# GLU products of a conformer and gMLP mixer in split float32r parts, their low parts made by VectorE between the taps of a depthwise convolution

## The reference

```python
z = h @ w_in + b_in
a = z[..., :2 * D_CONV]
uv = z[..., 2 * D_CONV:2 * D_CONV + 2 * D_GMLP]
gates = jax.nn.sigmoid(z[..., 2 * D_CONV + 2 * D_GMLP:])
a = jax.nn.glu(a, axis=-1)
a_full = jnp.concatenate([conv_hist.astype(a.dtype), a], axis=1)
...
a = jax.nn.silu(layer_norm(depthwise_causal_conv(a_full, conv_w, conv_b), ln_g, ln_b))
y_a = a @ w_a
uv = jax.nn.gelu(uv)
u, v = uv[..., :D_GMLP], uv[..., D_GMLP:]
v = layer_norm(v, v_ln_g, v_ln_b)
y_b = spatial_gate(u, v, w_s, b_s) @ w_b
merged = gates[..., :D_MODEL] * y_a + gates[..., D_MODEL:] * y_b
```

## Time and profile before

| | before |
|---|---|
| median of 3 runs | 967.47 us (964.45 to 967.98) |
| the profiled execution: span from first to last instruction | 963.2 us |
| mean granted TensorE clock, share of full speed | 0.940 |
| TensorE busy (matmuls) | 845.6 us, 88% of the span |
| VectorE busy | 509.0 us, 53% |
| ScalarE busy | 190.9 us, 20% |
| GpSimd busy | 168.8 us, 18% |
| 240 taps of the convolution (line 1280) | 175.1 us of VectorE |
| 512 plain GLU products (line 552) | 119.1 us of TensorE |

### The profile page before, as it was taken

The page is one execution under the profiler, slowest core; times in us unless marked ns, Lnnn a source line. Parts: engine busy times, 40 slices in busy tenths (PEclk is TensorE's granted clock), DMA queues, the critical chain, the costliest instruction groups (busy, mean ns, idle before and its releaser), DMA issues. The chain is left out here.

```text
span 963.2 us, 12133 instructions
## 1 busy us (share of the span) xinstructions
PE 845.6 (88%) x4994; PEld 618.5 (64%) x4994; DVE 509.0 (53%) x753; ACT 190.9 (20%) x284; POOL 168.8 (18%) x156
## 2 busy tenths in 40 slices
PE   2899999999998879979999999917999987979776
PEld 1688886347997879978878644605666655545432
DVE  1328999999999443351365543481333331222236
ACT  3211211111233121741120011201111110101003
POOL 1000000000045454143223000001122221121110
PEclk9899999999998889989999999856999998989899
DMA  9923225011332131365999593242999999999936
GB/s 323 315 64 88 65 67 174 1 44 44 89 88 57 48 88 45 88 219 175 316 314 322 186 381 149 97 193 83 411 404 416 415 418 394 368 406 394 373 110 248
DMA packets 112600, 204.16 MB, mean 212 GB/s; under 512 B 9484, under 2 KB 68212, under 8 KB 104350
## 3 DMA queue, kind: packets, MB, share of 16 engines
q1 hardware_dynamic: 94192, 159.36, 46.5%
q10 hardware_dynamic: 12830, 34.93, 9.6%
q0 software_dynamic: 5520, 9.06, 2.5%
HBM read 199.49 MB, written 14.84 MB: 223 GB/s over the span
## 5 line engine op out<-in xcount | busy, mean ns | idle before, releaser
L858 PE MATMUL PS<-arena 128*64 128x256 f32 (+1 forms) x1056 | 148.7, 411 | 30.2 <-issue 25.7
L1280 DVE SCALAR_TENSOR_TENSOR arena<-arena,VT 128x574 f32<-128x574 f32 x240 | 175.1, 811 | 0.0
L858 PEld LDWEIGHTS PS<-arena 128*64 128x64 f32 (+1 forms) x1056 | 108.8, 156 | 65.4 <-issue 36.9
L1695 POOL TENSOR_TENSOR wL<-arena,wH 128x1024 fp32r<-128x1024 f32 x32 | 83.2, 2621 | 360.8 <-ACT wH L998 360.8
L552 PE MATMUL PS<-arena 128*128 128x272 f32 x512 | 119.1, 396 | 1.6 <-DVE arena L1242 1.6
L552 PEld LDWEIGHTS PS<-arena 128*128 128x128 f32 x512 | 98.3, 192 | 22.1 <-issue 1.6
L619 PE MATMUL PS<-gH,wH 128*128 128x272 f32 x384 | 83.0, 299 | 9.1 <-POOL wL L1695 5.5
L1591 DVE TENSOR_TENSOR arena<-PS,arena 128x256 f32<-128x256 f32 x19 | 8.1, 424 | 140.1 <-ACT arena L1114 140.1
L619 PE MATMUL PS<-gL,wH 128*128 128x272 f32 x384 | 81.9, 296 | 0.0
L619 PE MATMUL PS<-gH,wL 128*128 128x272 f32 x384 | 81.7, 294 | 0.0
L878 PE MATMUL PS<-arena 128*64 128x512 f32 (+1 forms) x264 | 69.1, 597 | 1.4 <-DVE arena L1595 1.4
(11 more groups left out here) (282 smaller groups left out, 996.9 us busy)
## 6 DMA issues: line engine op xcount, KB each, us to landing
arena<-w_gate SPq DMA_DIRECT2D x32, 1024.0 KB, 7.3
arena<-w_up SPq DMA_DIRECT2D x32, 1024.0 KB, 15.4
arena<-w_down ACTq DMA_DIRECT2D x28, 1024.0 KB, 13.9
arena<-w_in SPq DMA_DIRECT2D x40, 512.0 KB, 5.2
arena<-w_ada SPq DMA_DIRECT2D x8, 2048.0 KB, 14.4
vecs<-w_ada SPq DMA_DIRECT2D x4, 2048.0 KB, 9.3
arena<-x_prompt SPq DMA_DIRECT2D x8, 512.0 KB, 8.0
arena<-w_in SPq DMA_DIRECT2D x4, 1024.0 KB, 6.3
```

The costliest lines, as they stand in the source:

```text
L858: last = pe.matmul(PS[h * rows:(h + 1) * rows, 2, n * DE:(n + 1) * DE], hG[:, b, k * SLOTS + h * rows:k * SLOTS + (h + 1) * rows], buf[r / ...
L1280: dve.scalar_tensor_tensor(out=total, in0=src, scalar=tap, in1=total, op0=ALU.mult, op1=ALU.add).then_inc(conv_step, 1)
L1695: pool.tensor_tensor(wL2[q % 2][:, m], WP[q % 2][:, m], wH2[q % 2][:, m], ALU.subtract).then_inc(gw_split, 1)
```

## The change

The GLU units become split products like the u units. ScalarE makes their weight high parts (high_of with the new semaphore a_high) and VectorE their low parts (low_a, a_split). VectorE now scales all eight tiles of hT, and the input's high parts (ScalarE) and low parts (VectorE) are made at the start, tile by tile; TensorE's unit 0 follows them step by step. The low parts of units 3 to 7 stand at fixed taps of the convolution's first pair (A_AT), those of the u units at fixed taps of pairs 4 and 6 (U_AT). The scratch row of the bias split moves to another buffer.

```diff
             for n in range(KT):
                 b = n % 2
-                full(pe, U_A + n)
                 pe.wait_ge(act_drained, Q_A + n - 1)
-                for m in range(2):
-                    last = product(4 * b + 2 * m, WP[b][:, m], hT, first=(n == 0))
+                if n == 0:
+                    for m in range(2):
+                        pe.wait_ge(a_split, m + 1)
+                    for k in range(KT):
+                        pe.wait_ge(g_high, k + 1)
+                        for w, part in ((wH2, gH), (wL2, gH), (wH2, gL)):
+                            if part is gL:
+                                pe.wait_ge(g_split, k + 1)
+                            for m in range(2):
+                                for h in range(2):
+                                    last = pe.matmul(PS[:, 2 * m + h, 0:H], w[0][:, m, k, :], part[:, k, h * H:(h + 1) * H],
...
+                else:
+                    for m in range(2):
+                        pe.wait_ge(a_split, 2 * n + m + 1)
+                        last = product_split(4 * b + 2 * m, wH2[b][:, m], wL2[b][:, m], gH, gL)
                 last.then_inc(w_used, 1)
...
-            act.wait_ge(s1_ready, 1)
-            for j in range(1, KT, 2):
...
+            def high_of(n, signal):
+                full(act, n)
+                for m in range(2):
+                    act.activation(wH2[n % 2][:, m], WP[n % 2][:, m], ACT.Copy).then_inc(signal, 1)
+
+            high_of(U_A, a_high)
+            for j in range(KT):
+                act.wait_ge(h_scaled, 2 * j + 2)
+                act.activation(gH[:, j, :], hT[:, j, :], ACT.Copy).then_inc(g_high, 1)
...
+            high_of(U_A + 1, a_high)
             act.wait_ge(start_dr, 3)
             act.wait_ge(aF_written, 4)
             for n in range(KT):
...
-                if n == 2:
-                    act.wait_ge(h_even, KT)
-                    act.wait_ge(h_odd, KT)
-                    act.wait_ge(bias_split, 3)
-                if n in (2, 3, 4, 5):
-                    for j in (2 * n - 4, 2 * n - 3):
-                        act.activation(gH[:, j, :], hT[:, j, :], ACT.Copy).then_inc(g_high, 1)
...
+                if n < KT - 2:
+                    high_of(U_A + n + 2, a_high)
...
+            def low_h(j):
+                dve.wait_ge(g_high, j + 1)
+                dve.tensor_tensor(gL[:, j, :], hT[:, j, :], gH[:, j, :], ALU.subtract).then_inc(g_split, 1)
+
+            def low_a(n):
+                for m in range(2):
+                    dve.wait_ge(a_high, 2 * n + m + 1)
+                    dve.tensor_tensor(wL2[n % 2][:, m], WP[n % 2][:, m], wH2[n % 2][:, m], ALU.subtract).then_inc(a_split, 1)
+
+            scale_h(0)
+            low_a(0)
+            scale_h(1)
+            for j in range(KT):
+                if j + 2 < KT:
+                    scale_h(j + 2)
+                low_h(j)
+            low_a(1)
...
+            low_a(2)
+            A_AT = {5: 3, 12: 4, 18: 5, 25: 6, 30: 7}
+            U_AT = {(4, 14): 0, (4, 24): 1, (6, 4): 3}
             for i in range(0, KT, 2):
+                if i == 6:
+                    low_u(2)
...
-                    if i == 6 and k in (9, 17, 25):
-                        low_u((k - 1) // 8)
-                if i == 2:
-                    dve.wait_ge(g_high, KT)
-                    for j in range(KT):
-                        dve.tensor_tensor(gL[:, j, :], hT[:, j, :], gH[:, j, :], ALU.subtract).then_inc(g_split, 1)
-                if i == 4:
-                    low_u(0)
+                    if i == 0 and k in A_AT:
+                        low_a(A_AT[k])
+                    if (i, k) in U_AT:
+                        low_u(U_AT[i, k])
```

More of the change, by code:

```diff
@@ L190, in build @@
         mg, sqj = tmp2[:, 0, 0:D], tmp2[:, 1, 0:D]
+        piece = mg[0:1, :]
         histR = tmp2[:, 1, 0:D]
@@ L545, in _ @@
         def _(pe):
-            def product(bank, tile_w, act, first=False):
-                for k in range(KT):
-                    if first:
-                        pe.wait_ge(h_odd if k % 2 else h_even, 2 * (k // 2 + 1))
-                    for h in range(2):
-                        last = pe.matmul(PS[:, bank + h, 0:H], tile_w[:, k, :], act[:, k, h * H:(h + 1) * H],
-                                         start=(k == 0), stop=(k == KT - 1))
-                return last
             pe.wait_ge(consts, NCONST)
@@ L625, in _ @@
                 b = n % 2
-                full(pe, U_A + n)
                 pe.wait_ge(act_drained, Q_A + n - 1)
-                for m in range(2):
-                    last = product(4 * b + 2 * m, WP[b][:, m], hT, first=(n == 0))
+                if n == 0:
[9 more added lines that the diff above has]
+                                    last = pe.matmul(PS[:, 2 * m + h, 0:H], w[0][:, m, k, :], part[:, k, h * H:(h + 1) * H],
+                                                     start=(k == 0 and w is wH2 and part is gH), stop=(k == KT - 1 and part is gL))
+                else:
+                    for m in range(2):
+                        pe.wait_ge(a_split, 2 * n + m + 1)
+                        last = product_split(4 * b + 2 * m, wH2[b][:, m], wL2[b][:, m], gH, gL)
                 last.then_inc(w_used, 1)
@@ L1239, in _, with scale_h @@
             dve.wait_ge(xt_copied, TT)
-            for j in range(0, KT, 2):
+            def scale_h(j):
                 for s, (c0, c1) in enumerate(((0, NPROMPT), (NPROMPT, T))):
                     dve.tensor_scalar(hT[:, j, c0:c1], hT[:, j, c0:c1], S1[:, s, j:j + 1],
-                                      VT[:, COL_MOD + 2 * j + s:COL_MOD + 2 * j + s + 1], ALU.mult, ALU.add).then_inc(h_even, 1)
+                                      VT[:, COL_MOD + 2 * j + s:COL_MOD + 2 * j + s + 1], ALU.mult, ALU.add).then_inc(h_scaled, 1)
+            def low_h(j):
[13 more added lines that the diff above has]
+            low_a(1)
             dve.wait_ge(bc_in, 64)
             then(dve.memset(b3, 0.0))
-            rest, piece = bvb[0:1, :], mod1[0:1, 0:D]
+            rest = bvb[0:1, :]
             for r in range(3):
```

24 lines of the change are left out of this document (9 added, 15 removed).

## The result

Four runs of the changed kernel gave a median of 988.15 us (985.83 to 989.42), four of the kernel before 967.73 us (964.45 to 969.45). The ratio is 1.0213, with a 95% interval of 1.0189 to 1.0236. The prediction was 986.8 us (975 to 992), slower.

A forecast was written before the change was run, and what follows sets the result against it. VectorE's gapless stream was taken to bound the kernel from 75 to 317 us. Terms 4.6 + 11.35 - 5.17 + 4.3 + 4.2 gave +19.3 us, span 982.5, plus 4.3 to the median: 986.8 us, range 975 to 992.

The forecast's parts named there:

- TensorE's gain: GLU units on TensorE: each falls from 14.9 to 12.1 us, 22 us over eight units, which TensorE then waits away.
- Rival (c): Whole kernel: not slower, TensorE sets the end and its lead comes through, 957.6 us; chance 0.05.
- The start: Up to the first GLU products: unit 1 comes late, so the convolution begins at 79.7 instead of 75.06, +4.6 us.
- The step that I weighed most: ScalarE's queue at the start: eight DMA issues, 8.9 us, delay unit 1's high part; TensorE idles 4.3 us.
- rival (b): Start: ScalarE's DMA issues hold nothing up, convolution begins 6 to 7 us earlier, about 980 us; chance alone 0.10.
- The five pieces: First pair of VectorE's convolution: low weights of units 3 to 7 between the taps, 2.27 us each, +11.35 us.
- The inputs' low parts: Between the second and third pair of the convolution: they leave VectorE's stretch there, -5.17 us.
- The waits: VectorE at u units 1 to 3: waits for ScalarE's high parts, 2.2, 0.6 and 1.5 us, together +4.3 us.
- GpSimd beside the additions: After the taps: four held GpSimd products meet VectorE's additions, 13.84 us instead of 9.65, +4.2 us.
- Rival (a): Convolution: GpSimd's products are done beneath the taps at no cost to VectorE, 978.5 us; chance 0.17.
- What TensorE gains before 290 us, it waits away: TensorE up to the mixes: it runs ahead of VectorE, so its gains there end in waits; no size of its own.
- the distance of 4.3 us between span and median: Whole kernel: the median 967.47 lies 4.3 us above the profiled span 963.2; kept, it turns 982.5 into 986.8.

The follow-up runs named there:

- E10: Changed kernel with GLU units 3 to 7 as plain products again, without the five low-weight pieces, u places at later taps; 969.54 us, ratio to before 1.0035.
- E1: Changed kernel with ScalarE's eight DMA issues behind unit 1's weight high parts instead of ahead of them; 977.29 us, ratio to before 1.0110.
- E5: Kernel before, plain GLU products kept, only the input's high and low parts made at the start; 967.37 us, ratio to before 1.0002.
- E9: E5 with the four u units' low parts at taps 1, 13, 20 and 27 of the last pair; 963.30 us, ratio to before 0.9953.
- E4: Changed kernel with the low parts of u units 1, 2 and 3 at later taps; 980.95 us, ratio to before 1.0163.
- E2: Changed kernel without GpSimd's low parts for gate units 0 and 1, ScalarE writing weight copies in their place; 980.72 us, ratio to before 1.0145.
- E7: E6 with gate unit 0's low part made by VectorE behind its additions instead of by GpSimd; 959.11 us, ratio to before 0.9915.
- E8: Changed kernel with the edits of E1 and E4 together; 977.04 us, ratio to before 1.0103.
- E6: Kernel before with input parts made at the start, only GLU units 1 and 2 split, u places 1 to 3 one tap later; 959.68 us, ratio 0.9927.
- E3: Changed kernel with GLU unit 5's low part made by GpSimd instead of VectorE; 1005.3 us in one run.

## Why the prediction was right

The direction, the size and the mechanism held, and the terms can be read one by one.

- **TensorE's gain is hidden.** The drains lie 12.10 us apart, as the prediction has it, and TensorE is 15 us less busy. E10 gave five of those GLU units their old length back and got faster. Rival (c) falls. (The 512 plain products of line 552 in the table of before are records: the program has 32 products per unit, 256 in all, and the trace shows two records for each.)
- **The start: +4.6 predicted, +4.85 measured.** The gap before unit 1 was 4.91 us (4.3 predicted), the clock was at 0.50 until 70.3. The step that I weighed most, the DMA issues, is shown by E1: with them out of the way the start shrinks by 7.68 us, a little more than the 6 to 7 of rival (b), which falls. The releaser in the row of that gap is VectorE's low part, not ScalarE's high part as I had said; the low part itself waited 8.02 us for the high part. That the sum came within 0.25 us is in part luck, since the same start took 37.94 to 40.20 us in five profiles. The first GLU products came at 81.51 instead of 79.7 because the scale factors were 1.60 us late, which the change does not touch.
- **The five pieces: +11.35 predicted.** The first pair took 57.49 - 46.15 = 11.34 us longer. E10 takes them out with the waits and gets 210.38 - 193.78 = 16.60 us back in the taps; 11.35 + 4.95 make 16.30. No run took them out alone.
- **The inputs' low parts: -5.17.** They are gone from the taps, as predicted. But by themselves they are worth nothing (E5), for the places behind them are tuned to TensorE's pace; with later places they are worth 0.5% (E9).
- **The waits: +4.3 predicted, 2.72 + 0.74 + 1.49 = 4.95 measured,** at the u units named. E4 removes them and gains 5.24 us in the taps.
- **GpSimd beside the additions: +4.2 predicted, +4.05 measured.** E2 shows the other end, 5.50 us alone, where I had estimated 5.6. Rival (a) falls: of the first product next to nothing was done beneath the taps, since 2.16 us of it were left when the additions began, and a product alone takes 2.37. Nor did products break in between the taps, for +6.9: the last 52 taps ran at 37.90 / 52 = 0.729 us.
- **The mean, the mixes:** the wait before the second mix is again 3.81 us, the first 0.93.

Four terms of the forecast came within 0.7 us. Two steps were too simple. "What TensorE gains before 290 us, it waits away" is right for a gain, but the reverse does not hold: E7, E9 and E10 show waits of 2 to 6 us at the square root, for ScalarE's queue, which TensorE paces by way of the weight loads. In the kernel before, this queue had 1.43 us to spare. What VectorE gains beyond that, or TensorE loses, TensorE decides (E9 gained 4.05 us in the taps and lost 2.14 there). And I kept the distance of 4.3 us between span and median for what lies around the span. In the runs made since, time less span was 1.7 to 1.9 us; so by that the profiled execution of before was itself some 2.5 us faster than the median. With 1.8 in its place the forecast would have been 984.3, so 2.5 us of its closeness rest on that distance. The measured median lies 20.4 us above that of before, for a sum of 19.3. The span differs by 24.4, since the profile of after has the late scale factors and 2.4 us more behind the mix, neither of which the sum had. And what came after the mix was taken as unchanged; that holds only to within the 2 us or so by which this part differs between profiles (E8).

## What to carry to other kernels

Before a matmul is made cheaper by work on another engine, find the engine whose stream has no gaps in that stage, and price the new work there: here TensorE was busy 15 us less and VectorE paid 11.35 us for it, in the stretch where it has no gap. Take the part that fits into that engine's idle time (E6), and look at what the moved step is queued behind: eight DMA issues in front of one high part cost 7.7 us here. Pieces at fixed places in one engine's stream are tuned to another engine's pace; whoever shifts one of the streams has to set the places anew before judging the shift (E5 and E9).

## What was not expected of the hardware

- A GpSimd product (2.37 us each where two ran while VectorE waited, 4.74 us at 288.02 in E10) stood 27.7 us behind VectorE's taps (from 264.23 to 291.89), and in E3 for about 15. In the changed kernel it came in when VectorE changed from taps to additions. In E3 it did not come in at the change from taps to a weight piece (124.09) but at the change back to taps (126.36). From there on the two took turns (in E3 two taps of 2.90 and 2.91 us, each beside a product).
- Two of the eight DMA issues on ScalarE's queue, for the router's w_re (128x8x32) and b_rg (128x4), took 2.16 and 3.49 us to issue in the changed kernel; the other six took 0.36 to 0.65.
- In E1 an activation ran at 53.35 beside the issue of 53.19, which lasts 0.94 us: here activations that stand ahead of the issues in the program were not held up by them. Those behind were: the next one came at 62.76, after the last issue.
